# Two groups of small products per mixing iteration issued one weight tile later, in groups that already stand there

## What is computed

```
h = rmsnorm(x, norm_mix)
z = h @ w_in                       # q, k, v, qg, kg, vg, rg, ag, ga, gb
oa = attend(rope(qa), rope(ka), va, lam)     # two softmax maps per head, A1 - lam*A2
og, S = recur(qg, kg, vg, g)                 # gated linear attention in chunks of 64
ua = rmsnorm(oa, a_subln) @ w_pa
ub = (rmsnorm(og, g_norm) * silu(rg)) @ w_pb
x = x + (sigmoid(ga) * ua + sigmoid(gb) * ub) @ w_o
x = x + (silu(h @ w_f1) * (h @ w_f3)) @ w_f2
x = x + sigmoid(h @ w_ple_gate) * (pe @ w_ple)
```

## Time and profile before

| what | value |
|---|---|
| median of 3 runs | 1484.67 us |
| the profiled execution's own time | 1482.29 us |
| span of that execution | 1480.5 us |
| TensorE busy (matmul) | 1389.2 us, 94% |
| VectorE busy | 885.2 us, 60% |
| ScalarE busy | 621.6 us, 42% |
| GpSimd busy | 248.8 us, 17% |
| mean granted TensorE clock | 0.973 of full speed |
| data moved | 191.67 MB, mean 129 GB/s |

### The profile page before, as it was taken

The page is one execution under the profiler, slowest core; times in us unless marked ns, Lnnn a source line. Parts: engine busy times, 40 slices in busy tenths (PEclk is TensorE's granted clock), DMA queues, the critical chain, the costliest instruction groups (busy, mean ns, idle before and its releaser), DMA issues.

```text
span 1480.5 us, 24169 instructions
## 1 busy us (share of the span) xinstructions
PE 1389.2 (94%) x9814; PEld 1338.4 (90%) x9814; DVE 885.2 (60%) x1471; ACT 621.6 (42%) x1040; POOL 248.8 (17%) x289
## 2 busy tenths in 40 slices
PE   5999998999999999999979999899899999999996
PEld 2899897999899999999868999889889999999995
DVE  3666756577656655545557576565765655555554
ACT  3445342534744433333344535344474443334332
POOL 1303020030005000022431030302100310001233
PEclk9999998999999999999989999999999999999998
DMA  7555598764344454444536657986434454454443
GB/s 160 106 118 132 115 100 107 136 124 128 100 143 144 148 165 143 145 157 150 136 65 114 136 120 122 103 101 141 105 102 155 141 160 143 143 171 137 144 148 71
DMA packets 195210, 191.67 MB, mean 129 GB/s; under 512 B 9078, under 2 KB 192188, under 8 KB 195100
## 3 DMA queue, kind: packets, MB, share of 16 engines
q1 hardware_dynamic: 189904, 181.62, 53.2%
q0 software_dynamic: 2688, 7.35, 1.3%
q10 hardware_dynamic: 2508, 1.16, 0.3%
HBM read 181.45 MB, written 8.65 MB: 128 GB/s over the span
## 4 chain that ended last, share of the span: by engine, by line
PE 67%; DVE 11%; DMA 10%; POOL 5%; issue 4%; ACT 3%; SPq 0%; DVEq 0%; POOLq 0%; ACTq 0%
PE big L1172 20%; PE big L1174 19%; PE big L1173 19%; DMA w_raw<-in_w_in 9%; DVE w_lo L824 3%; POOL E L514 2%; POOL rot L521 1%; POOL E L515 1%; PE X L1435 1%; PE X L1213 1%; ACT w_hi L546 1%; PE X L1335 1%; DVE E L1005 1%; DVE E L1004 1%; DVE ssq L956 1%
## 5 line engine op out<-in xcount | busy, mean ns | idle before, releaser
L1172 PE MATMUL big<-x_hi,w_hi 128*128 128x320 f32 x1984 | 634.2, 320 | 21.6 <-DVE z L902 13.3
L1173 PE MATMUL big<-x_lo,w_hi 128*128 128x320 f32 x1984 | 619.4, 312 | 0.0
L1174 PE MATMUL big<-x_hi,w_lo 128*128 128x320 f32 x1984 | 619.4, 312 | 0.0
L824 DVE TENSOR_TENSOR w_lo<-w_raw,w_hi 128x1024 fp32r<-128x1024 f32 (+1 forms) x330 | 416.8, 1266 | 158.1 <-ACT w_hi L546 156.1
L546 ACT CAST w_hi<-w_raw 128x1024 fp32r<-128x1024 f32 x328 | 329.9, 1035 | 200.7 <-DMA w_raw<-in_w_in 107.6
L1172 PEld LDWEIGHTS big<-x_hi,w_hi 128*128 128x128 f32 x1984 | 379.1, 191 | 32.9 <-DVE z L902 15.4
L1173 PEld LDWEIGHTS big<-x_lo,w_hi 128*128 128x128 f32 x1984 | 379.3, 191 | 2.1
L1174 PEld LDWEIGHTS big<-x_hi,w_lo 128*128 128x128 f32 x1984 | 378.2, 191 | 0.0
L478 POOL TENSOR_TENSOR sqt<-xT 128x320 f32<-128x320 f32 x48 | 52.8, 1100 | 619.7 <-DVE xT L1121 421.4
L1172 PE MATMUL big<-h_hi,w_hi 128*128 128x320 f32 x352 | 108.6, 309 | 0.0
L1173 PE MATMUL big<-h_lo,w_hi 128*128 128x320 f32 x352 | 108.4, 308 | 0.0
(11 more groups left out here) (226 smaller groups left out, 1741.7 us busy)
## 6 DMA issues: line engine op xcount, KB each, us to landing
w_raw<-in_w_in SPq DMA_DIRECT2D x130, 512.0 KB, 8.5
w_raw<-in_w_f SPq DMA_DIRECT2D x120, 512.0 KB, 4.5
w_raw<-in_w_pb SPq DMA_DIRECT2D x16, 512.0 KB, 4.5
w_raw<-in_w_pa SPq DMA_DIRECT2D x16, 512.0 KB, 4.0
w_raw<-in_w_o SPq DMA_DIRECT2D x16, 512.0 KB, 4.4
w_raw<-in_w_ple_gate SPq DMA_DIRECT2D x16, 512.0 KB, 4.6
w_raw<-in_w_f SPq DMA_DIRECT2D x16, 384.0 KB, 3.4
k_raw<-in_cache_k SPq DMA_DIRECT2D x8, 256.0 KB, 9.7
```

The costliest lines, as they stand in the source:

```text
L824: tt(w_lo[:, t % 4, 0:nk, :], w_raw[:, (t // 2) % 2, 0:nk, (t % 2) * P:(t % 2 + 1) * P], w_hi[:, t % 4, 0:nk, :].bitcast(F32), ALU.subtrac ...
L1172: mm(out, wh, xh[:, k0 + k, :], start=start and k == 0, stop=False)
L1173: mm(out, wh, xl[:, k0 + k, :], start=False, stop=False)
L1174: last = mm(out, wl, xh[:, k0 + k, :], start=False, stop=stop and k == nk - 1)
```

## The change

Of TensorE's groups, the one after T9 (the transposes of vgT and `att_transposes(0)`) goes behind T10, ahead of the group that stands there; the one after T12 (`values(0)` and `own_sums`) goes behind T13, ahead of the group that stands there. Every wait moves with its products. Nothing is added or removed, and the programs of the other four engines stay as they are.

```diff
-                    if t == 9:
+                    if t == 10:
                         pe.wait_ge(probs_ready, at(10, 5))
                         transposes(X[5], vgT[:, 0, :]).then_inc(vg_trans, 1)
                         transposes(X[0][:, P:4 * P], vgT[:, 1, :])
                         att_transposes(0)
-                    if t == 10:
                         pe.wait_ge(a_ready, at(3, 2))
                         pe.wait_ge(result_read, rb + (10 + CREDIT_RES))
                         for h in range(2):
                             transposes(X[1 + h], vz[:, h, :]).then_inc(v_trans, 1)
                         pe.wait_ge(a_ready, 3 * v)
                         transposes(X[3], E[:, NL, :]).then_inc(k_trans, 1)
-                    if t == 12:
+                    if t == 13:
                         pe.wait_ge(v_copied, 4 * v)
                         pe.wait_ge(v_past_in, 16 * v)
                         values(0, X[1])
                         pe.wait_ge(k_copied, 7 * v)
                         own_sums()
-                    if t == 13:
                         att_transposes(1)
                         mm(X[5][:, 0:GDV], kdT[:, 2, :], vg_tok[:, 2, :], start=True, stop=True).then_inc(u_done, 1)
```

## The result

The changed kernel takes 1486.97 us, median of 20 runs (1482.70 to 1491.44); the kernel before took 1480.99 us in the 20 runs that it was compared with (1478.06 to 1486.76). The ratio is 1.0037, 95% interval 1.0026 to 1.0048: slower by 5.5 us, 3.9 to 7.1. Two further comparisons of the same kernel gave 1.0051 (1.0033 to 1.0069) and 1.0054 (1.0036 to 1.0071), +7.5 and +8.0 us. The forecast was +3.9 us, to 1488.2, with a range of 1484 to 1494.

A forecast was written before the change was run, and what follows sets the result against it. TensorE, busy 94% of the span, was taken to bound the kernel, so its order counts through idle time and switching costs. Iteration losses of 2.25 and 1.68 gave +3.9 us, to 1488.2 us; range 1484 to 1494.

The forecast's parts named there:

- The covered wait: T9 to T10: moved group no longer covers T10's wait for VectorE's reading of T8; T11 starts at 18.35, losing 0.85 or 0.94 us.
- both kinds of iteration: Iterations like 1 (3, 5, 6): T9 ends at 11.25 us behind pair products; like 2 (4, 8): 9.74; bank free about 12.0.
- the sum: Iterations 1, 5, 6 give 2.25 us, 4 and 8 give 1.68, 2, 3, 7 give 0: +3.9 us; chance 0.55.
- The number of waits: Ahead of T10: seven waits for T8's reading, three to four near 0.75 us, three near 2.3, some 9.7 in all.
- Iteration 7: At T10: no wait, since VectorE is done at 977.79, before T9 ends at 978.24; gain 0.1 us.
- The second move: Group from T12 to T13: T13 goes from 3.62 to 3.52 us with no new wait, -0.1 us in each iteration.
- The lateness behind the move: ScalarE's high part for T13 and the fetch into that buffer come about 1.1 us later; nothing waits for them.
- the four stretches of 35.4: From T15's end to the next pair products, four of six stretches start from T1 and carry TensorE's delay over in full.
- What arrives at the end: Losses of iterations 2, 3 and 7 are absorbed by waits for weights; the loss of iteration 6 shifts the whole stretch.
- The clock: New 2.26 us idles ahead of T10: falls cost about 1.7 us, even odds at two places, taken as cancelling a possible -1.7.
- the fall in iteration 3: T14 of iteration 3 ran at clock 0.56 behind 1.39 us idle; that idle shrinks to 0.8, so -1.7 us may come.
- the first rival: The clock falls in the new stalls: two to four falls at 1.7 us, +7.3 to +10.7, 1492 to 1495; chance 0.2.

The follow-up runs named there:

- Experiments 3 and 4: VectorE reads T8 ahead of the decay matrix's first part: 3 in the changed kernel, 1480.21 us (0.9992); 4 in the kernel before, 1480.37 us (0.9995).
- third profile of the change: Profile from the whole change measured again against the kernel before, in the same rounds as the kernel with the wait filled: 1489.26 us, 1.0054.
- the split kernel: Whole change, but the six vgT transposes stay behind T9, against the kernel before: 1480.31 us, 0.9995; a second time 1479.92 us, 0.9995.
- the filled kernel: Whole change, with the six vgT transposes also issued once uselessly behind T9 (0.65 us), against the kernel before: 1484.82 us, 1.0021.
- experiment 11: The kernel before against itself, nothing changed, with a second profile: 1479.95 us, 0.9995.
- experiment 1: Only the group behind T9 moves behind T10, the group behind T12 stays, against the kernel before: 1489.38 us, 1.0043.
- experiment 7: The kernel before with T8 read early and the transposes of E moved behind T11's scores, against the kernel before: 1479.16 us, 0.9988.

## Why the prediction was right, and which step was off

**The covered wait: right.** The claim was that VectorE's chain frees the bank at 12.0 us behind the pair products in both kinds of iteration, so that T10 stands still there and the moved group is added behind it, T11 at 18.35. Measured 18.31 to 18.34 in the first two profiles, and 18.29 to 18.40 in the third where the clock did not fall in T10. Two small errors in the sum cancel: T10 takes 3.62 us (84.31 to 87.93) in place of 3.73, the joined group 2.69 (87.93 to 90.62) in place of 2.62. Experiments 3 and 4 show the cause: making the reading early takes the loss away, and does nothing without the move.

**The number of waits: nearly right.** Seven waits were forecast with 9.7 us, and the first profile has seven with 4.3. The reason is that in the first profile the clock fell at the pair products in all eight iterations, so that TensorE came late to the end of T9 and waited for 0.57 to 0.72 us in each but the seventh. In the first profile of before three iterations were of the other kind. In the third profile of the change there are waits of 2.08 to 2.09 in three iterations and 8.1 us in all. Which kind an iteration is does not belong to the kernel but to the execution (in the kernel before it was iterations 2, 4 and 8 in the first profile and 5, 6 and 8 in the second); I had taken the kinds of one execution for fixed.

**Iteration 7: wrong in kind.** I gave it no wait, since T9 ended at 978.24, behind the reading. In the first profile of the change T9 ended early enough that T10 started at 12.0 there too, without a recorded wait. No price hung on it, since the sum has this iteration at 0.

**The second move: right in the rows, not measurable.** T13 takes 3.52 us in place of 3.62, but from T11 to T14 it takes 16.08 in place of 16.14, so only 0.06 of the 0.1 arrives; the time of that move alone is 1.0007 (0.9986 to 1.0027).

**The lateness behind the move: mis-sized for ScalarE, and without a price where it could be seen.** Counted from the pair products in iteration 1, the high part for T13 came at 18.54 in place of 14.14, 4.4 us later and not 1.1. T13's low part and the fetch behind it did come 1.1 us later. T13 starts at 26.98, long after, and the distances from T11 to T14 and from T15 to the next pair products have not grown, so in the four stretches of 35.4 it costs nothing. Into iterations 3 and 7, where the weights set the pace, no run moves the fetch alone.

**What arrives at the end: partly right, partly open.** The distance from T15 to the next pair products stayed at 35.4 us where it was forecast to, so columns 1, 4 and 8 of the table show the full 0.8. The distance from iteration 2 to 3 did not grow in the first profiles (89.38 and 88.97), but in the kernel before it was 88.21 the second time and in the change 89.27 and 88.91, so one profile cannot tell an absorbed 0.8 us from chance. From iteration 6 to 7, where the sum let the loss through, it was 90.15 and 89.85 before, and 90.69, 91.30 and 91.20 with the change. In iteration 3 the wait for the maps of head 1 shrank from 1.39 to 0.37, as forecast (0.8 or gone):

```profile
276.66 0.33 PE L1260 MATMUL X<-cst,p 128*128 128x128 f32 x1 [0.37 <-DVE dmat L940]
```

The 4.9 us between the filled and the split kernel, at 0.65 us each, would be seven or eight iterations; the difference of the ratios gives 3.8 us, with an uncertainty of some 2.5. A part of it is not stall at all: the filled kernel's profile has a fall of the clock in T15 of iteration 7 (see below) that neither profile of the split kernel has, and from that iteration to the next it takes 85.96 us for 84.36 and 83.77. Whether iterations 2, 3 and 7 absorb their share of the loss stays open; the sum took all three as absorbed.

**The clock: the step that failed.** The prediction took the fall of the clock in the new waits "with even odds at each of the two places that count", set it against the fall in iteration 3 that might go, and said "I take these as cancelling". They did not cancel. The gain was there: with the change no profile has the fall in iteration 3, as said under experiment 11. The new falls outweighed it. A wait of 2.1 us ahead of T10 was followed by a fall in six of seven cases over the profiles (all four of experiment 1, two of three in the third profile of the change), at about 1.5 us each (19.8 against 18.3). It came in iterations 1, 4, 5 and 8, not only in the two places that were counted. Filling 0.65 us of the wait gave 4.4 us back. So the first rival was not a separate case but a part of the likeliest one: without the falls at T10 the kernel is 3.1 us above before (the filled kernel, 1.5 to 4.9), near the plain sum of 3.9, and the clock there adds another 2.4 to 4.9 us, depending on the comparison. Those 3.1 us are not the stall alone: the filled kernel's profile has the fall in T15 of iteration 7, and not the one in iteration 3. The range held, since the rival was in it.

**The number: closer than the sum deserved.** 1488.2 stands on a time before of 1484.3, and the kernel before took 1480.99 in its 20 runs, 3.3 less. The change by the medians is 6.0 us, 2.1 more than the sum. The two errors have opposite signs, so that the forecast lies only 1.2 us from the measured 1486.97; that closeness is luck.

The Trainium skill (TensorE: Matmul & The Clock Gate, "HAM oscillation — how this bites in real kernels") would have left the clock alone at these waits, and the sum as it stood: the six falls behind 2.1 us of idle time and the filled kernel disagree. The section of the same page of the Trainium skill on a second failure mode, by which frequent short idles between groups of matmuls let the clock go back and forth, fits these rows better; no run here varied how often such idles come.

One thing remains unexplained. In iteration 7 TensorE waits for ScalarE's copy of the maps ahead of `values(1)`, and in T15, right behind, the clock fell in three of three profiles of the change and in that of the filled kernel; of the ten other profiles one had a fall there (experiment 7). In the first profile of the change:

```profile
1010.47 0.38 PE L1274 MATMUL X<-attT,v_tok 128*128 128x128 f32 x1 [1.95 <-ACT attT L653]
```

```profile
1011.80:1015.40 3.60, 3.60 (x16) 3.60 (x16) 2.02 (x3) 3.35 (x8) 1.09 (x2) 0.53 0.58 155
```

The kernel before waited there for 2.40 us in its first profile and T15 ran at the full clock:

```profile
1012.10:1015.70 3.60, 3.60 (x26) 3.60 (x26) 2.00 (x3) 3.34 (x8) 1.09 (x2) 1.00 0.53 135
```

The wait was longer there and the clock stayed up, so the length of one wait does not decide by itself. What TensorE did some microseconds earlier is different (T10 to T14 stand otherwise), but no run here takes that apart.

## What to carry to other kernels

Ahead of moving work out of a place because no wait shows there, look up when the next instruction could have started at all: here the bank came free 0.7 to 2.2 us after T9's end, so that 0.7 us of the 1.72 us of small products, or all of them, cost nothing where they stood. A wait that shows as 0.5 us behind a filler is as long as the filler and more once the filler is gone. Where an idle stretch of TensorE cannot be avoided, try leaving some work in it, even work that could go elsewhere: about half of this loss went when 0.65 us of useless products stood in the wait. And compare several executions: what the clock does differs between executions of one program, and two profiles of the kernel before lay 3.8 us apart.

## What the runs showed of the hardware

With 2.1 us of idle time ahead of a tile the granted clock fell in that tile in six of seven cases; with 1.42 to 1.44 us at the same place (four cases, in the split and the filled kernels) it fell in none, and with 0.03 to 0.86 us in none. Most of these last had the fall at the pair products already, so they say less about the length. The 2.2 us ahead of the pair products, the same in all kernels (iterations 3 and 7 have more), was followed by a fall in some iterations and not in others of one and the same program. Where it fell there, with the change, it was hidden behind VectorE's chain (T11 at 18.33 with it and at 18.29 without), and no second fall came in T10. So at these two places an iteration had one fall or none, and with the change one at T10 cost 1.5 us where one at the pair products cost nothing.
